# Delta rule in a hybrid decoder step: four more places of dense work ahead of the first inverse level in two tiles

## The reference, cut to what matters

```python
proj = h @ w_in                      # 24 chunks of 128 columns
qkv_c = silu(short_conv(qkv))        # chunks 0 to 11
A = where(strict, einsum(kb, k) * decay, 0)
sol = triangular_solve(I + A, rhs)   # per tile and head: the inverse
v_new = u - wk @ S
o = qd @ S + qk @ v_new              # the state S goes from tile to tile
S = S * gl + kd.T @ v_new
```

## Time and profile before

| | us |
|---|---|
| median of 3 runs | 2651.72 (2650.94 to 2652.86) |
| profiled execution, its own time | 2652.95 |
| its span in the trace | 2651.1 |
| PE busy in the span | 2584.7 (97%) |
| DVE busy, ACT busy | 1381.5, 1127.6 |

### The profile page before, as it was taken

One profiled execution on the slowest core, in us unless ns is written; L12 is line 12 of the kernel. 1 busy time (PEld: TensorE's weight loads), 2 busy tenths in 40 slices (PEclk: granted clock), 3 DMA queues, 4 the chain that ended last, 5 costly groups with the idle time before them and its releaser, 6 DMA issues.

```text
span 2651.1 us, 39320 instructions
## 1 busy us (share of the span) xinstructions
PE 2584.7 (97%) x16324; PEld 2308.4 (87%) x16324; DVE 1381.5 (52%) x2201; ACT 1127.6 (43%) x1914; POOL 243.7 (9%) x396
## 2 busy tenths in 40 slices
PE   9998989999999999999999999999999999999998
PEld 7778878788887798899999989998877888999998
DVE  4746764656564465434444465535544456454344
ACT  6654446455444245333333345433332345333324
POOL 4121111100101001100000001110000000000000
PEclk9999999999999999999999999999999999999999
DMA  7453335533333445543333245554434343233322
GB/s 204 157 158 104 105 106 140 154 97 89 106 91 95 119 144 164 173 121 112 104 95 111 83 132 152 162 149 123 120 119 150 97 121 122 85 112 107 96 88 82
DMA packets 368721, 321.47 MB, mean 121 GB/s; under 512 B 11929, under 2 KB 339667, under 8 KB 368544
## 3 DMA queue, kind: packets, MB, share of 16 engines
q1 hardware_dynamic: 336224, 207.91, 27.2%
q0 software_dynamic: 32320, 111.05, 13.8%
HBM read 261.33 MB, written 57.58 MB: 120 GB/s over the span
## 4 chain that ended last, share of the span: by engine, by line
PE 86%; DVE 6%; ACT 5%; DMA 2%; issue 1%; SPq 0%; DVEq 0%; ACTq 0%
PE dense L605 76%; PE mixer L605 8%; ACT arena L1148 1%; DVE wlo L1665 1%; ACT whi L1148 1%; DMA wst<-in_w_in_even_dram 1%; DVE arena L1890 0%; DMA arena<-xrow 0%; ACT relu L1148 0%; DVE hf L1806 0%; DMA xrow<-arena 0%; ACT L1148 0%; ACT L1153 0%; DVE arena L1892 0%; DVE hlo L1802 0%
## 5 line engine op out<-in xcount | busy, mean ns | idle before, releaser
L605 PE MATMUL dense<-hhi,whi 128*128 128x272 f32 (+1 forms) x3072 | 848.2, 330 | 16.8 <-DVE wlo L1665 11.2
L605 PE MATMUL dense<-hhi,wlo 128*128 128x272 f32 (+1 forms) x3072 | 825.3, 323 | 0.0
L605 PE MATMUL dense<-hlo,whi 128*128 128x272 f32 (+1 forms) x3072 | 825.1, 323 | 0.0
L1665 DVE TENSOR_TENSOR wlo<-wst,whi 128x1024 fp32r<-128x1024 f32 x384 | 472.1, 1229 | 235.0 <-ACT whi L1148 234.1
L1148 ACT ACTIVATE whi<-wst 128x1024 fp32r<-128x1024 f32 x384 | 403.9, 1052 | 419.4 <-PE dense L605 407.9
L605 PEld LDWEIGHTS dense<-hhi,whi 128*128 128x128 f32 x3072 | 515.4, 189 | 72.7 <-DVE wlo L1665 16.4
L605 PEld LDWEIGHTS dense<-hhi,wlo 128*128 128x128 f32 x3072 | 514.4, 189 | 41.8
L605 PEld LDWEIGHTS dense<-hlo,whi 128*128 128x128 f32 x3072 | 516.4, 189 | 37.3 <-issue 0.7
L605 PE MATMUL dense<-h1hi,whi 128*128 128x272 f32 (+1 forms) x1536 | 423.0, 330 | 9.4 <-DVE wlo L1665 5.0
L605 PE MATMUL dense<-h1hi,wlo 128*128 128x272 f32 (+1 forms) x1536 | 414.5, 324 | 0.0
L605 PE MATMUL dense<-h1lo,whi 128*128 128x272 f32 (+1 forms) x1536 | 412.7, 323 | 0.0
(11 more groups left out here) (352 smaller groups left out, 1814.5 us busy)
## 6 DMA issues: line engine op xcount, KB each, us to landing
wst<-in_w_ff_dram SPq DMA_DIRECT2D x256, 512.0 KB, 3.9
wst<-in_w_in_even_dram SPq DMA_DIRECT2D x48, 512.0 KB, 4.1
wst<-in_w_in_odd_dram SPq DMA_DIRECT2D x48, 512.0 KB, 4.0
proj<-ffh POOLq DMA_DIRECT2D x48, 272.0 KB, 2.6
proj<-ffh POOLq DMA_DIRECT2D x48, 256.0 KB, 2.3
arena<-proj POOLq DMA_DIRECT2D x16, 512.0 KB, 4.8
wst<-in_w_out_even_dram SPq DMA_DIRECT2D x16, 512.0 KB, 4.0
arena<-proj POOLq DMA_DIRECT2D x8, 1024.0 KB, 8.1
```

What stands on the lines that cost most here:

```text
L605: return pe.matmul(out, lhsT, rhs, start=start, stop=stop)
L1665: TT(wlo[:, u % 2, :], wst[:, u % 2, :], whi[:, u % 2, :].bitcast(F32), ALU.subtract)\
```

## The change

```diff
-            out += [("rest",)] * 1 + [("g", t, s, 0) for s in ("b1", "b2", "b3")] + [("rest",)] * 5
+            out += [("rest",)] * 1 + [("g", t, s, 0) for s in ("b1", "b2", "b3")] + [("rest",)] * (9 if t in (1, 3) else 5)
             out.append(("g", t, "b4", 0))
```

## The result

| | before | after |
|---|---|---|
| median (15 runs each) | 2651.86 (2649.75 to 2655.03) | 2656.82 (2654.08 to 2660.15) |
| profiled execution, its own time | 2652.95 | 2657.71 |
| its span | 2651.1 | 2655.9 |
| PE busy | 2584.7 | 2585.0 |

A forecast was written before the change was run, and what follows sets the result against it. PE, busy 2584.7 of 2651.1 us, bounds the kernel, so only its waits and clock count: 24.7 waits + 4.0 clock - 25.0 before = +3.7 us, 2656.6 profiled, median 2655.4; range 2646 to 2661.

The forecast's parts named there:

- Tile 1, early: `sum` goes ahead of chunk 1's low weight; PE's `dec` newly waits 2.5 us, and A ends at 216.3, before 215.4.
- Tile 1, blocks: `b4` comes at 239.4 again with one more place done; waits 2.1 and 2.9; gain 1.5 us and the clock.
- Tile 2: `la` 4 waits 3.9 us, `dec` 0.95, `lb` 4 0.35; tile 2 takes 1.9 of what tile 1 gave.
- Tile 3: Blocks end early, but `b4` waits for chunk 11's weight; waits: `la` 4 5.9 us, chunk 12 4.0, `lb` 4 1.1, `vT` 1.0.
- The clock: Low PE clock behind waits costs 4.0 us after the change (bounds 1.5 and 8), as before it.
- rival C: Clock falls only behind the long waits, 3.9 and 5.9, costing 3.2 us; +2.9, so 2654.6 us; chance 0.10.
- rival B: Low clock after each of the four new waits that count, 8 to 9 us in all; 2660 us; chance 0.28.
- Rival A: Places simply fill the waits of tiles 1 to 3: -6.2 us, and -4.0 of low clock; 2641.5 us; chance 0.14.
- the ring: Tile 3: chunk 8's store goes behind L2534, delaying ACT's high weight, DVE's chunk 11 low weight and `b4`; PE waits 5.9 us.

The follow-up runs named there:

- sum behind: Kernel after, but DVE takes `sum` of tile 1 behind the low weight of chunk 1; median 2655.81 us, ratio 1.0011 to the kernel before.
- store first: Kernel after, but POOL issues chunk 8's store ahead of `b3` of tile 3 (L2532, L2534); median 2651.33 us, ratio 0.9993 to the kernel before.
- the store behind: Also the last kernel: nine rests in tiles 1, 2, 3 (2645.66 us), but POOL issues `b3` of tile 3 ahead of chunk 8's store; 2649.74 us.
- Tile 1 alone: Kernel before with the nine rests in tile 1 only; median 2659.46 us, ratio 1.0025 to the kernel before.
- rests 7, 9, 7: Kernel after, but 7, 9, 7 rests in tiles 1, 2, 3 and DVE's `sum` of tile 1 behind chunk 1's low weight; 2653.71 us, ratio 1.0005.
- before again: The unchanged kernel before, run and profiled a second time; median 2651.79 us, ratio 0.9996.
- after again: The changed kernel, run and profiled a second time; median 2655.94 us, ratio 1.0016 to the kernel before.

## Why the prediction was right

It said +3.7 us and a median of 2655.4; measured were +4.2 (2.6 to 6.1) and 2656.82. Of the waits it had 24.7 us, the trace has 23.0 (before 21.0); of the clock 4.0, and it is 4.15. That makes +2.2 in the stretch of this profile; the second profile of each kernel gives +5.2 for place 0 to `oT`, where the first gives +2.4. The mean of the two, 3.8, fits the times. But that each term came out so near is luck of this one profile: the second has 18.5 us of waits and 10.5 of clock, which is above the bound of 8. What held in both is the total, 28.7 forecast, 27.2 and 29.0 measured. (The forecast's own timeline has about 1 us less than its list of waits, by roundings in tiles 2 and 3.) Point by point, times of after less the 2.8 us of start-up:

- *Tile 1, early*: `dec` goes on at 210.0 with a wait of 2.31 (predicted 209.9 and 2.5), and A ends at 216.3, as predicted. Held; sum behind shows that `sum`'s place makes about half of the wait.
- *Tile 1, blocks*: the mis-sized step. `b4` was to come "at 239.4 again" and comes at 242.2. The parts: 0.5 was lost in my own addition (A's end + 0.3 + 4.9 + 2.3 is 223.8, not 223.3); A's store is issued 1.06 behind A in place of 0.3, because two chunk stores stand ahead of it on POOL (218.26 and 219.64); the blocks take 0.25 more; and from L2534 to L1972 it is 5.34 us (239.70 to 245.04) where the earlier trace rows have 4.12. So the wait for chunk 3's weight is 1.94 (2.1), but ahead of `la` 4 it is 3.92 (2.9), and chunk 21's weight adds 1.36 that was not in the sum. Five us of waits became 7.2. `la` 4 comes 2.8 us later with one place more done: ahead of it tile 1 lost 1.3 us where I had a gain of 1.5. The second profile repeats it: from L2534 to L1972 5.12 us, and `la` 4 52.6 us behind place 0 (52.7; before 49.9 and 49.2).
- *Tile 2*: `la` 4 waits 1.75 in place of 3.9, `dec` 0.61 (0.95), `lb` 4 0.23 (0.35), `vT` 0.76 (not foreseen). From `la` 4 of tile 1 to that of tile 2 it is 57.8 us (57.1 predicted, 59.1 before), so the chain was right. The wait is shorter mainly because 1.7 us of low clock lie in this stretch, which I had counted apart from it.
- *Tile 3*: the blocks end, the store goes behind L2534, lands in 4.13 (3.9), and the weight stands ahead of `b4`. `la` 4 comes 43.2 us after `o` of tile 2 begins (320.89 to 364.11); predicted 44.1. Waits: chunk 12 3.27 (4.0), `la` 4 5.64 (5.9), `vT` 0.72 (1.0). `lb` 4 has no wait (1.1): `la` 4 ran at half clock and covered its mask. Counted from `o`, every step held, and store first and the store behind show the cause by moving one step on POOL each way. On the clock of the whole kernel all of it comes 2.5 us later than written (`la` 4 at 361.3, not 358.8), because tile 1 was late.
- *The clock*: after the waits of 1.36, 1.94 and 3.92 low clock came only at 246.14, after those of 1.75 and 3.27 none, after 5.64 at once. So in this profile only the two longest waits were followed by it, as rival C has it, but at 4.15 us, the size of the forecast (C: 3.2). In the second profile it fell behind waits of 2.31, 1.92, 2.49 and 1.55 too, which is rival B's mechanism, without B's 2660: the low clock behind the waits for weights runs inside a chain and shortens the wait at its end. Adding waits and clock as separate terms, as the forecast and B do, counts such a piece twice. Which of C and B a single execution follows is not settled by these runs. Rival A is refuted by the wait of 5.64 (4.11 in the second profile). With the ring taken away (store first) the time is that of before, which is still 10 us above A's 2641.5, so A's count of "two places further" was wrong beside the ring: it counts cover gained and forgets that the chains themselves are the length.

What was right for a wrong reason: the prediction has the change gain in tile 1 and lose in tile 3. Tile 1 alone, at +6.6 us, shows that this is not so. Each part alone loses. I had no step for that: tile 1 alone was expected at 0 to 3 us faster.

## What to carry to other kernels

Where the critical engine waits at the end of each pass for a chain through other engines and DRAM, count two things: the work left outside the chains, and the length of the chains; filler moved into a chain's cover gains only by what it takes out of the outside. For each moved step, list what it passes on every queue that issues it. Here a step of two small transfers that went ahead of one large store closed a ring POOL, ACT, DVE, PE that cost 4 to 5 us, and putting the store back ahead of it cost nothing that showed in the time. When a wait seems to hang on the place of one instruction, move that and see whether the next in line takes the wait over, as L1988 did. And profile a kernel twice before explaining a difference by single waits or by the clock: add waits and clock up over one stretch and compare the sums.

## What the runs showed of the hardware

- A chunk's store on POOL's queue lands in 2.46 us when it goes out ahead of the block traffic (352.46 to ACT's 354.92), and in 4.13 and 3.18 when it goes out right behind L2534 (354.75 to 358.88; 350.64 to 353.82). The 3.9 that I read off was such a pair. Whether L2534's small packets or the queue itself delays it was not tried.
- A low weight is 1.2 us, but 2.4 to 2.7 when POOL's `tensor_tensor` L2546 falls wholly inside it (2.39 in rests 7, 9, 7, where both start together at 339.03). The two in the last kernel:

```profile
334.85 2.67 DVE L1665 TENSOR_TENSOR wlo<-wst,whi 128x1024 fp32r<-128x1024 f32 x1 [2.03 <-ACT whi L1148]
...
335.13 1.30 POOL L2546 TENSOR_TENSOR arena<-arena 128x512 f32<-128x512 f32 x1
```

  In the kernel after, L2546 ran from 340.12 to 341.42 and overlapped the weight's first 0.3 us, and the weight took 1.37. The Trainium skill (GPSIMD Engine Reference, "1. Specifications") has POOL's SBUF interfaces shared with VectorE, with contention for DVE instructions with two SBUF inputs, which L1665 is; the trace agrees, and the loss, 1.2 to 1.5 us, is about POOL's 1.30. Whether it is a part of why the waits for chunk 12's weight differ by a microsecond between kernels was not tried.
- Low clock did not go by the length of the wait ahead: behind the same wait of 3.27 us for chunk 12's weight the first two matmuls took 0.52 us in the kernel after (353.69) and 0.82 in sum behind (352.48), and behind the same 2.69 us 0.52 in before (348.91) and 0.82 in before again (348.31), with PEclk 0.50 for 5.7 us. In after again it fell behind a wait of 1.55 us. Two profiles of one kernel differ by 1 to 2.5 us in one wait while their medians agree to 0.9: the differences of single waits below that size say nothing here.
